# Products of constants on TensorE ahead of the long waits of a fused eight-part network kernel

## The reference

```python
def rms_norm(x, gain):
    y = xf * lax.rsqrt(jnp.mean(xf * xf, axis=-1, keepdims=True) + EPS)
    return y * gain

def hybrid_layer(x, ...):                      # twice
    h = rms_norm(x, attn_pre_gain)             # stage n1
    u = h @ w_in
    ...                                        # two attentions, gates
    x = x + rms_norm(mixed @ w_out, attn_post_gain)   # n2
    h = rms_norm(x, ffn_pre_gain)              # n3
    x = x + rms_norm(conv_ffn(h, ...), ffn_post_gain) # n4
    return x

def second_block(x, ...):
    for layer in range(2):
        mix = gated_deltanet(h, ...) if layer == 0 else differential_attention(h, ...)
        h = layer_norm(ALPHA * h + mix, ...)   # l0, l1
        ffn = hierarchical_moe(h, ...)         # route, gather, experts, way back
        h = layer_norm(ALPHA * h + ffn, ...)   # m0, m1
    return h
```

## Time and profile before

| | |
|---|---|
| median of 3 runs | 3761.3 us (3761.04 to 3761.95) |
| the profiled execution's own time | 3760.82 us |
| its span, first to last instruction | 3759.0 us |
| PE busy | 3419.9 us (91%) |
| DVE, ACT, POOL busy | 2413.9, 1947.6, 284.5 us |
| granted TensorE clock, mean of the span | 0.946 |
| chain that ended last, share of PE | 84% |

### The profile page before, as it was taken

One profiled execution on the slowest core, in us unless ns is written; L12 is line 12 of the kernel. 1 busy time (PEld: TensorE's weight loads), 2 busy tenths in 40 slices (PEclk: granted clock), 3 DMA queues, 4 the chain that ended last, 5 costly groups with the idle time before them and its releaser, 6 DMA issues.

```text
span 3759.0 us, 52844 instructions
## 1 busy us (share of the span) xinstructions
PE 3419.9 (91%) x16584; PEld 2694.3 (72%) x16584; DVE 2413.9 (64%) x3619; ACT 1947.6 (52%) x3025; POOL 284.5 (8%) x307
## 2 busy tenths in 40 slices
PE   7899989996899989997989986999999699779996
PEld 5666768784766768786768874888888476568884
DVE  3677466723477556634656634899999446379995
ACT  3366443423266443423553334788887336358884
POOL 0000000000000000000014400111111000011110
PEclk9899999998899989998999996999999899889998
DMA  3211222221211212221210004999999221089994
GB/s 137 73 46 41 90 67 95 94 92 61 90 41 40 79 67 95 90 95 67 85 56 7 1 23 157 342 363 367 359 369 388 111 74 38 1 302 368 387 382 169
DMA packets 159936, 546.05 MB, mean 145 GB/s; under 512 B 27936, under 2 KB 27936, under 8 KB 158496
## 3 DMA queue, kind: packets, MB, share of 16 engines
q1 hardware_dynamic: 140256, 510.37, 37.4%
q0 software_dynamic: 16256, 16.84, 1.3%
q10 hardware_dynamic: 3264, 16.78, 1.2%
HBM read 547.02 MB, written 38.80 MB: 156 GB/s over the span
## 4 chain that ended last, share of the span: by engine, by line
PE 84%; DVE 6%; ACT 4%; issue 3%; DMA 1%; DVEq 0%; ACTq 0%; POOLq 0%; SPq 0%; POOL 0%
PE psum L690 23%; PE psum L692 22%; PE psum L691 22%; PE psum L959 3%; PE psum L735 2%; PE psum L804 2%; PE psum L837 2%; PE psum L1134 1%; PE psum L819 1%; PE psum L1097 1%; PE psum L1140 1%; DVE arena L2179 1%; ACT x L1526 1%; PE psum L1238 1%; DMA arena<-rows_out_m 1%
## 5 line engine op out<-in xcount | busy, mean ns | idle before, releaser
L2510 DVE TENSOR_TENSOR ew_r<-arena,ehigh_r 128x1024 fp32r<-128x1024 f32 x648 | 750.2, 1219 | 17.8 <-ACT ehigh_r L1723 17.5
L1723 ACT ACTIVATE ehigh_r<-arena 128x1024 fp32r<-128x1024 f32 x648 | 632.0, 1053 | 27.0 <-DMA arena<-in_moe_w 26.9
L1862 DVE TENSOR_TENSOR ring_rounded<-ring,highs 128x1024 fp32r<-128x1024 f32 x302 | 369.6, 1225 | 428.6 <-ACT highs L1311 428.0
L690 PE MATMUL psum<-oab_r,highs 128*128 128x512 f32 x1424 | 586.5, 412 | 44.1 <-DVE h_r L1877 17.5
L692 PE MATMUL psum<-oab_r,ring_rounded 128*128 128x512 f32 x1424 | 564.9, 397 | 0.0
L691 PE MATMUL psum<-h_r,highs 128*128 128x512 f32 x1296 | 512.4, 395 | 0.0
L1311 ACT ACTIVATE highs<-ring 128x1024 fp32r<-128x1024 f32 x302 | 318.0, 1054 | 341.4 <-PE psum L692 319.3
L690 PEld LDWEIGHTS psum<-oab_r,highs 128*128 128x128 f32 x1424 | 270.0, 190 | 141.2 <-DVE h_r L1877 38.3
L690 PE MATMUL psum<-ehigh_r,xT_high_r 128*128 128x512 f32 x864 | 352.3, 408 | 11.1 <-DVE xT_low_r L2514 6.3
L692 PE MATMUL psum<-ehigh_r,xT_low_r 128*128 128x512 f32 x864 | 341.3, 395 | 0.0
L691 PE MATMUL psum<-ew_r,xT_high_r 128*128 128x512 f32 x864 | 340.0, 393 | 0.0
(11 more groups left out here) (361 smaller groups left out, 6052.7 us busy)
## 6 DMA issues: line engine op xcount, KB each, us to landing
arena<-in_moe_w SPq DMA_DIRECT2D x648, 512.0 KB, 5.8
ring<-in_wstream SPq DMA_DIRECT2D x312, 512.0 KB, 3.3
rows_in_m<-arena ACTq DMA_DIRECT2D x4, 2048.0 KB, 9.5
arena<-rows_out_m ACTq DMA_DIRECT2D x8, 1024.0 KB, 7.9
x<-in_xT SPq DMA_DIRECT2D x1, 2048.0 KB, 10.9
result<-x SPq DMA_DIRECT2D x8, 256.0 KB, 2.1
const<-in_const SPq DMA_DIRECT2D x1, 1112.5 KB, 5.3
arena<-rows_in_m,arena POOLq DMA_INDIRECT x58
```

What stands on the lines that cost most here:

```text
L690: pe.matmul(acc, lhs[0], rhs[0], start=start, stop=False)
L1723: act.activation(ehigh_r[p], ew[:, p, :], ACT.Copy).then_inc(expert_cast[mi], 1)
L1862: dve.tensor_tensor(ring_r[:, c % R, :], ring[:, c % R, :], highs[:, c % HIGHS, :].bitcast(F32), ALU.subtract).then_inc(weights_split, seq ...
L2510: TT(ew_r[p], ew[:, p, :], ehigh_r[p].bitcast(F32), ALU.subtract).then_inc(expert_split[mi], 1)
```

## The change

A helper `idle_products(n, bank)` is added to PE's program. It issues n plain f32 products of the constant ones (128x128) with 512 columns of the constants, each into a PSUM bank that nobody reads afterwards before it is written again. They wait for nothing and signal nothing. It is called at fourteen places; the calls within the loop over layers run twice, those in `layer_norm_sums` four times, those in `experts` twice. Two waits are added in front of such calls, for `n4.rs` and for `dan.rs0`. Nothing is removed or moved.

```diff
+            def idle_products(n, bank):
+                for _ in range(n):
+                    pe.matmul(psum[:, bank, :], ones, const[:, 0:512], start=True, stop=True)
+
             pe.wait_ge(const_in, seq.at("const"))
+            idle_products(10, 5)
             pe.wait_ge(x_in, seq.at("x0"))
             with seq.loop("layer", LAYERS):
                 meet("n1")
                 column_sums("n1", sq)
+                idle_products(9, 5)
...
                 added_sums("n2", total)
+                idle_products(6, 5)
                 column_sums("n3", sq)
+                idle_products(9, 5)
...
                 pe.wait_ge(dve_done, seq.at("down.d7"))
+                idle_products(5, 7)
                 added_sums("n4", total)
+                pe.wait_ge(act_done, seq.at("n4.rs"))
+                idle_products(13, 7)
 
                 pe.wait_ge(dve_done, seq.at("n4.h0"))
                 for _ in range(LAYER_PAD):
...
             def layer_norm_sums(stage, sq, acc=None, banks=(7, 6)):
...
+                idle_products(2, 5)
                 column_sums(stage, sq, banks[1])
+                idle_products(10, 5)
...
                     .then_inc(pe_done, seq.step(f"{m}.jrow"))
+                idle_products(5, 2)
                 for n in range(2 * NT):
                     if n % NT == 0:
                         pe.wait_ge(dve_done, seq.at(f"{m}.hot{n // NT}"))
...
+                idle_products(10, 7)
                 pe.wait_ge(rows_gathered[mi], 32)
                 turn_x()
+                idle_products(2, 7)
                 pe.wait_ge(rows_high[mi], 1)
...
                 meet(f"{m}.back")
+                idle_products(12, 7)
                 for t in range(NT):
                     pe.wait_ge(dve_done, seq.at(f"{m}.yt{t}"))
...
             sums_of(SUMS[4:])
+            pe.wait_ge(act_done, seq.at("dan.rs0"))
+            idle_products(6, 4)
             pe.sem_inc(settled, 1)
             for r in range(8):
                 tile("wo2", r, (kda_r, oda_r), drained=dve_done, first="oo")
```

## The result

The kernel after takes **3734.4 us** (median of 4 runs, 3729.8 to 3735.8) beside 3761.6 us before on the same chip: a ratio of **0.9925** (95% interval 0.9909 to 0.9941), 27 us less. Its profiled execution took 3735.78 us with a span of 3734.0. The calls of `idle_products` stand at thirteen places, as the diff shows, and not at fourteen. The page of the profile first, then the table of windows.

A forecast was written before the change was run, and what follows sets the result against it. The prediction took PE to bound the kernel, slowed by a low clock after waits. Its terms summed to -24.1 us, from 3760.8 to 3736.7, with the median 0.5 above the profiled execution giving 3737 us; range 3726 to 3750.

The forecast's parts named there:

- n3: Norm in each layer: sum -0.4 and up's restart at the high clock -1.6, together -4.0 us for two layers.
- n4: Norm at each layer's end: 13 products overrun after a new 2.7 us idle stretch, +2.0 us per layer, bounds +0.3 and +3.1.
- l0 and l1: Norms ahead of the router: sums of squares of 9.94 and 8.83 us fall to 7.0 at high clock, -4.7 together.
- Router: Router's products begin high and end low, taking half of the possible gain: -3.4 us each, -6.8 together.
- Routing's tail: Five products ahead of `hot0` overrun their wait by 2.0 us, 16 later records need 1.8 less: +0.2 each, +0.4 together.
- Experts' start: Ten products fit into the gather's wait; transposes and first expert products run high: -2.2 us each, -4.4 together.
- Way back of m0: After the first expert stage: restart wins 1.6 us, sums that may start low cost 0.5: -1.1.
- m1: Way back of the second expert stage: possibly low-starting sums against a gain on other sums, 0.
- the clock holds better: Rival: n4's 2.7 us idling keeps the clock high and the router runs high throughout, 3726 us; chance 0.11.
- Weight loads set the pace: Rival: loads pace the small products whatever the clock, so router and L1122 gain nothing, 3747 us; chance 0.06.
- Bound by DMA: Rival: DMA bounds the expert stages, so the experts' start gains nothing (+4.4), 3741 us; chance 0.08.
- Blocks behind a wait stay low to their end: Rival: blocks starting on an idle PE stay at the low clock, result +41 us, 3802; chance 0.04.

The follow-up runs named there:

- e1_tiny: Kernel after with each added product 2 columns wide in place of 512: 3759.4 us, ratio to before 0.9994.
- e2_no13: Kernel after without the added wait for n4.rs and the 13 idle products behind it: 3730.0 us, ratio to before 0.9914.
- e5_direct: Kernel after with the 13 products waiting for the logarithm instead of the root, and two of the start's ten moved ahead of each n1 sum: 3731.3 us.
- e6_covers: e2_no13 with more waits covered (compression, ab, wo, experts' second batch) and block sizes changed behind the first expert stage, in routing and at wo2: 3712.4 us.
- e11_gather16: Kernel after with 16 idle products in place of 10 ahead of the gathered rows, too many on purpose: 3746.9 us, ratio to before 0.9962.
- e8_after_again: The kernel after, unchanged, measured again: 3735.3 us, beside 3760.8 us for the kernel before.
- e9_gather8: e6_covers with 8 idle products in place of 10 ahead of the gathered rows: 3714.6 us, ratio to before 0.9878.
- e10_covers2: e9_gather8 with 7 for 5 products in the compression, 3 for 4 at ab, 7 ahead of the delta rule's heads, 4 ahead of the first attention scores: 3713.4 us.
- e12_short_waits: e10_covers2 with 2 products in the wait ahead of each expert stage's last products and 1 ahead of each layer's branches: 3711.2 us.

## Why the prediction was right, point by point

Forecast 3737, range 3726 to 3750; measured 3734.4. Sign, mechanism and size held: `e1_tiny` shows that the gain hangs on wide products, and the clock column that it comes from TensorE's clock. That the total came out within 1 us (-25.0 between the profiled executions, forecast -24.1) is in part luck, since errors of up to 2.2 us of either sign cancel. By its steps, with the aligned differences:

- **Start** -2.3 and -1.6: measured -2.35 and -1.55. The ten products ended at 16.50 us and not at 17.5.
- **n3** -2.0 each: -1.65 and -1.80. The term that failed is n3's sum, -0.4: it takes 9.57 us, and the whole gain is up's restart.
- **n4** +2.0 each: from the n4 sum's start to the next stage's first product are 22.4 us (861.87 to 884.26) against 20.0 before in layer 0, and 20.8 (1731.81 to 1752.57) against 19.0 (1737.29 to 1756.26) in layer 1: +2.4 and +1.8 (+2.2 and +1.7 aligned). The clock did fall behind the new wait of 2.72 us, for 3.4 us, and PE, no longer DVE, set the layer's end, as foretold. `e2_no13` and `e5_direct` confirm both halves.
- **n1 of layer 1, ab**: -1.6 and 0; -1.7 and -1.0 +1.0.
- **l0 and l1** -4.7: -2.80 and -1.88.
- **Router** -3.4 each: -2.57 and -2.90. Half of the difference between low and high was too much: 64 records took 11.30 and 10.97 us. The estimate left out the transposes behind them, which took 6.32 and 4.99 us against 5.42 and 5.53 before.
- **Routing's tail** +0.2 each: from the job row (L1131) to the end of L1137 are 9.04 and 9.38 us against 9.16 in both before, -0.1 and +0.2.
- **Experts' start** -2.2 each: -2.7 and -3.9. In m1 the clock held over the uncovered wait of 3.13 us and in m0 it fell, as in both before; the prediction took 0.3 off for both.
- **Way back of m0** -1.1: -0.3. The first sum started low, but it had done so before too (7.69 and 7.61 us), so the +0.5 for that is not there. The step that failed is the restart, -1.6: it (2968.00, clock 0.61) lost most of its gain behind a wait of 2.33 us that ten products left open. `e6_covers` closed it with two more and had 1.5 us.
- **m1** 0: -2.2, the largest error of a place. **wo2** -2.0: -2.6.
- **Not in the prediction at all**: the code that the change doesn't touch. Waits of 2.2 to 2.4 us at 1237 and 1852 us, behind which the clock had held before, now brought it down: +1.35 and +1.58; in other places -1.43 and +0.6. Together that is +2.1 us, which the sum put at nothing; it cancels against m1 by luck.

Of the rivals, *the clock holds better* was wrong in both of its places. *Weight loads set the pace* fell: the 16 records of L1137 took 1.88 us after and 3.65 before, the same products and weight loads at the other clock level. The rule of the Trainium skill (TensorE: Matmul & The Clock Gate, section LDWEIGHTS) that had spoken for it gives one rate, columns over 1.2 GHz. The trace doesn't agree: PEld was busy 3.49 us with these loads at the low clock and 1.75 at the high one. *Bound by DMA* fell by `e11_gather16`. *Blocks behind a wait stay low to their end* was right only in part in routing (5.1 of 7.1 us low in m0, 5.8 of 7.4 in m1) and wrong for the gather (8.82 us for ten), wo2 and n4 (3.4 us low each).

## What to carry to other kernels

Work for its own sake on TensorE pays where a wait ends in wide products, if it stands directly behind the last real work, ends just before the operands come, and leaves no wait of 2 us or more at either side: over waits of 2.0 to 3.2 us the clock held in some executions and fell in others. The same blocks of 2 columns brought nothing (`e1_tiny`); widths between 2 and 512 weren't tried as such blocks. Count the block at the low clock as well as at the high one, because products that run past the end of the wait are paid in full (`e11_gather16`), and a block whose start moves can become the bottleneck of the place it was to help. Judge an edit of 1 to 2 us by the aligned traces place by place, since the total carries the chance of every short wait in the rest of the kernel.

## What the runs showed of the hardware that was not expected

**The same wait costs the clock in one execution and not in the next.** The wait of 2.21 us ahead of m0's last expert products left the clock high in the kernel after, `e2_no13` and `e6_covers`, and low behind it, for 3.41 us, in `e8_after_again` (the same code as the kernel after), `e9_gather8` and `e10_covers2`; waits of 2.16 to 2.36 and of 3.13 us did likewise. Each time 1.4 to 1.6 us hang on it. The trace before shows it already: of its four waits of 2.08 us ahead of a sum of squares, two left the clock high (m0 and m1, 7.13 us each) and two did not (l0 and l1, 9.94 and 8.83 us), so that what the prediction read from one of them, that the clock holds over 2.08 us, was half of it. The Trainium skill (TensorE: Matmul & The Clock Gate, section What's actually happening) says that the number of slow products of one kernel varies from run to run with the phase of the clock's control at the kernel's start. These traces agree that it varies, at waits in the middle of the kernel too; that the phase decides it no run here shows. What decides it in a given execution wasn't tried and stays open. Whether it is also why the kernel after spreads over 7.5 us isn't shown: `e12_short_waits`, with two of these waits covered, stayed within 2.5 us, but so did `e11_gather16`, with none of them covered (2.1 us in five runs).

**A block of fixed work has no fixed duration.** The ten products ahead of the gather took 8.82 us in the kernel after, and 10.52 and 11.76 in `e6_covers`, where they began 1.7 us earlier and the clock fell under them; the sixteen of `e11_gather16` took 15.50 us in m0 and 13.97 in m1 of one execution. So a gain of 1.7 us in routing was largely taken back by the block behind it.
